# Moving VectorE's low-part subtraction to an earlier place within an attention step

## The chip, the cores and the metric

The kernel runs on 1 core of a Trainium2 chip. The metric is the device time of one launch in microseconds (us). The shown time is a median of 3 runs. The profile is of one further execution, with its own time.

## What is computed

The reference is two blocks of two layers each on one sequence of 512 positions, width 1024, in float32. Three of its attentions matter here, since the same class of the kernel computes all three:

- the sparse attention of the first block's second layer: 16 heads of 64, causal, with a mask made by a top-128 choice and a relative bias; its output is multiplied by silu(z);
- the sliding-window attention of the second block's first layer: 16 heads, window 128, with sinks;
- the second block's second layer, where two attentions of 16 heads (selected blocks, which here are all of them, and a window of 512) are added with gates to a compressed one.

```python
def attention(q, k, v, bias, mask):
    s = einsum(q, k) + bias
    s = where(mask, s, NEG_INF)
    p = softmax(s)
    return einsum(p, v)
...
x = x + (out * gate) @ w_out
```

Each output is then the input of a projection, `@ w_out`. The kernel keeps float32 precision in that projection by splitting a tile x into a rounded high part (`hi`, type fp32r) and a low part `lo = x - hi`, and by adding three products: hi times the weights' low part, lo times their high part, hi times their high part.

## The kernel before

The program is written engine by engine. Each stage is a class with one method per engine (`on_pe`, `on_dve`, `on_act`, `on_pool`, `on_sp`), and the five instruction streams meet only at semaphores. An engine takes its own stream strictly in the order in which it is written, so a wait holds back all that stands behind it on that engine.

The class `Attention` is used three times. In this text its uses are called the causal block (it writes `odd_hi`, `odd_lo`; 641 to 721 us of the trace), the windowed block (`win_hi`, `win_lo`; 822 to 881 us) and the two-branch block (`long_hi`, `long_lo`; 1393 to 1531 us). The 16 heads are taken in 8 pairs (m = 0 to 7), the 512 queries in 4 tiles of 128 in the order t = 3, 1, 2, 0. One pair and one query tile (and one branch) is a step s: 32 steps in the causal and the windowed block (4 a pair), 64 in the two-branch block (8 a pair). How many keys a step reads goes by its tile: 512, 256, 384 and 128 for t = 3, 1, 2, 0 in the causal and two-branch blocks, at most 256 in the windowed one.

The engines run a software pipeline over the steps. A step's work is, in order:

- PE `score(s)` (line 2000; mask added by line 1997): two heads' scores into one of two pairs of banks. It waits for the logits of step s-2.
- DVE `logit(s)` (line 2068; with sinks a small copy first, line 2065): scores plus bias from the bank into a probability buffer, with the row minimum.
- ACT `exp(s)` (line 2161), then DVE `share(s)` (line 2074, a reciprocal), then POOL `divide(s)` (line 2133).
- PE `turn(s)` (line 2014), three steps later: transposes of the probabilities. It waits for POOL.
- `keep(s)`: the transposed probabilities from the bank to SBUF, on ACT (line 2170) for even steps, on DVE (line 2096) for odd ones; in the two blocks with more than 256 keys DVE takes the rest of the even ones (line 2098).
- PE `mix(s)` (line 2031), five steps later: probabilities times values into bank 7. It waits for `finish(s-1)`, since all steps use the same bank for their sum.
- DVE `finish(s)` (lines 2084, 2086, 2088), six steps later: the sum is read from bank 7 and put into the output tile `out(m)`.
- ACT `split_high(m)` (line 2174), after the last `finish` of the pair: `hi(m) = round(out(m))`.
- DVE `split_low(m)` (line 2102), one step later on DVE: `lo(m) = out(m) - hi(m)`. It waits for `split_high(m)`.

With the constants FINISH = 6, HIGH = 6 and LOW = 7, `split_low(m)` stands in DVE's step s = 10 + 4m of the causal and windowed blocks and s = 14 + 8m of the two-branch block. In that step DVE's stream also has `finish(s-6)`, `logit(s)` of a tile t = 2, `share(s-1)` and `keep(s-3)`, and the next step begins with `finish(s-5)`, for which PE's `mix(s-4)` waits. Steps from 32 (64) on have no logit; only the splits of m = 6 and m = 7 lie there in the first two blocks, and only that of m = 7 in the third. ACT's step 9 + 4m is `exp`, `keep`, `split_high(m)`.

The waits that carry this text:

```python
# PE, mix(s)
pe.wait_ge(self.outs.sem, self.outs.at(s if s < self.NS - 3 else s - 1))
# DVE, split_low(m)
dve.wait_ge(self.high.sem, self.high.at(m + 1))
# ACT, split_high(m)
act.wait_ge(self.outs.sem, self.outs.at(self.per_pair * (m + 1)))
```

The `lo` tiles are read only by the output projection behind the block (`part_ready`), whose first products start at the end of the block.

Of the kernel before, what the change touches and what calls it, by code (L numbers as in the profile page):

```python
# [76 lines left out]
class Stage:  # L77
# [11 lines left out]
    def on_dve(self, dve):  # L89
        pass  # L90
# [1815 lines left out]
class Attention(Stage):  # L1906
# [144 lines left out]
    def on_dve(self, dve):  # L2051
        nc, steps, keys, st, pad = self.k.nc, self.steps, self.keys, self.st, self.pad

        def logit(s):
            m, t, e = steps[s]
            nk = keys(t)[1]
            pr, b = self.probs_of[s % 4], self.bias_of(s)
            if self.bias is not None and s % self.per_pair == 0:
                dve.wait_ge(self.landed[m % 2].sem, self.landed[m % 2].at((m // 2 + 1) * 16))
            if t in self.pooled:  # L2060
                dve.wait_ge(self.added.sem, self.added.at(2 * m + t))
            dve.wait_ge(self.turned.sem, self.turned.at(s - 3))
            dve.wait_ge(self.scores.sem, self.scores.at(s + 1))
            if self.sink is not None:
                nc.vector.tensor_copy(pr[:, :, 0], self.sink[:, 2 * m:2 * m + 2])
            for x in range(2):
                first = -CUT if self.sink is None else self.sink[:, 2 * m + x:2 * m + x + 1]
                nc.vector.tensor_tensor_reduce(out=pr[:, x, pad:pad + nk], in0=self.S(s, x)[:, 0:nk], in1=b[:, x, :],  # L2068
                                               scale=1.0, scalar=first, op0=ALU.add, op1=ALU.min,
                                               accum_out=st[:, s % 4, 0, x:x + 1]).then_inc(self.logits.sem, 1)  # L2070

        def share(s):
            dve.wait_ge(self.probs.sem, self.probs.at((s + 1) * 2))
            nc.vector.reciprocal(st[:, s % 4, 2, :], st[:, s % 4, 1, :]).then_inc(self.dens.sem, 1)  # L2074

        def finish(s):
            m, t, e = steps[s]
            r = slice(t * P, (t + 1) * P)
            o = self.out(m)[:, r]
            dve.wait_ge(self.mixed.sem, self.mixed.at(s + 1))  # L2080
            if self.finishing is not None and s % self.per_pair == 0:
                self.finishing(dve, m)
            if self.add:
                nc.vector.tensor_tensor(o, self.O(s), o, ALU.add).then_inc(self.outs.sem, 1)
            elif self.times is not None:
                nc.vector.tensor_tensor(o, self.O(s), self.times(m)[:, r], ALU.mult).then_inc(self.outs.sem, 1)
            else:
                nc.vector.tensor_copy(o, self.O(s)).then_inc(self.outs.sem, 1)

        def keep(s):  # L2090
            blocks = keys(steps[s][1])[2]
            r, w = blocks[0][1], 2 * P * len(blocks)
            dve.wait_ge(self.mixed.sem, self.mixed.at(s - 1))
            dve.wait_ge(self.turned.sem, self.turned.at(s + 1))
            if s % 2 == 1:
                nc.vector.tensor_copy(self.turned_of[1][0:r, 0:w], self.T[1][0:r, 0:w]).then_inc(self.kept[1].sem, 1)
            else:
                nc.vector.tensor_copy(self.turned_of[0][0:r, 512:w], self.T[0][0:r, 512:w]).then_inc(self.rest.sem, 1)

        def split_low(m):  # L2100
            dve.wait_ge(self.high.sem, self.high.at(m + 1))
            nc.vector.tensor_tensor(self.lo(m), self.out(m), self.hi(m).bitcast(F32), ALU.subtract).then_inc(self.low.sem, 1)

        for s in range(self.NS + self.LOW):
            if 0 <= s - self.FINISH < self.NS:
                finish(s - self.FINISH)
            if s < self.NS:
                logit(s)
            if 0 <= s - 1 < self.NS and not (self.trail and s == 2):
                share(s - 1)  # L2110
            if self.first_dve is not None and s < 2:
                self.first_dve(dve, s)
            if self.trail and s == 1:
                share(1)
            if self.trail and s == 2:
                self.before.evict(dve, "dve", self.before.tiles - 1)
            if 0 <= s - self.TURN < self.NS and (self.halves or (s - self.TURN) % 2 == 1):
                keep(s - self.TURN)
            done = s - self.LOW + 1
            if done > 0 and done % self.per_pair == 0:  # L2120
                split_low(done // self.per_pair - 1)

    def on_pool(self, pool):
        nc, steps, keys, pad = self.k.nc, self.steps, self.keys, self.pad
# [1019 lines left out]
```

## Time and profile before

| what | value |
|---|---|
| median of 3 runs | 1942.56 us (1942.49 to 1942.62) |
| the profiled execution's own time | 1942.33 us |
| its span, first to last instruction | 1940.5 us |
| granted TensorE clock, mean | 0.999 |
| PE busy | 1910.1 us, 98% |
| DVE busy | 1071.6 us, 55% |
| ACT busy | 770.6 us, 40% |
| POOL busy | 333.0 us, 17% |
| DVE line 2102, causal block | 8 times, median 872 ns |
| DVE line 2102, windowed block | 8 times, median 692 ns |
| DVE line 2102, two-branch block | 8 times, median 682 ns |

PE, PEld, DVE, ACT and POOL are TensorE's matmuls, its weight loads, VectorE, ScalarE and GpSimd. Busy shares are means over the whole span; in a timeline, a row's start plus its duration can lie up to some 0.1 us behind the start of the next row on the same engine, because the next instruction enters before the last has left. Times in brackets behind a row are the engine's idle time before it and who ended it. The profiled execution lies 1.8 us above its span and 0.2 us below the median of the runs.

### The profile page before, as it was taken

To read this page: it belongs to the slowest core of one execution; us is meant where nothing else is said; L and a number is where in the kernel's file an instruction comes from. 1 tells how busy PE (TensorE), PEld (TensorE's weight loads), DVE (VectorE), ACT (ScalarE), POOL (GpSimd) and SP (SyncE) were. 2 spreads that over 40 slices of the span, in tenths; PEclk is the share of its full clock that TensorE was granted. 3 is DMA by queue.
4 is the path that set the end of the run, shared out by engine and by line. 5 is a ranking of instruction groups with operands and counts; after the bars stand their busy time and mean duration, and the time that the engine had idled before them with its cause. 6 is when DMAs were issued, how large, how long until landed. Compare 5 with 4: busy or idle time off the path is not lost.

```text
span 1940.5 us, 25271 instructions
## 1 busy us (share of the span) xinstructions
PE 1910.1 (98%) x9688; PEld 1505.5 (78%) x9688; DVE 1071.6 (55%) x2029; ACT 770.6 (40%) x1407; POOL 333.0 (17%) x419
## 2 busy tenths in 40 slices
PE   9999999999999999999999999999999999999998
PEld 7887778888777668758888888888766788888886
DVE  5576644444699765485544443353788654544323
ACT  4343333432454654474322222232567442222213
POOL 0640000001130751051000000030256310000002
PEclk9999999999999999999999999999999999999999
DMA  9452324443323123312333333365100133333332
GB/s 206 135 171 75 101 85 152 141 152 86 101 68 104 47 56 87 93 50 87 98 96 95 95 96 94 101 172 171 44 2 1 45 98 96 100 98 98 98 98 77
DMA packets 297246, 187.67 MB, mean 97 GB/s; under 512 B 32543, under 2 KB 274719, under 8 KB 296870
## 3 DMA queue, kind: packets, MB, share of 16 engines
q1 hardware_dynamic: 288958, 168.02, 30.6%
q10 hardware_dynamic: 8168, 18.03, 2.4%
q8 instruction: 78, 1.28, 0.3%
q14 instruction: 42, 0.34, 0.1%
HBM read 183.79 MB, written 17.96 MB: 104 GB/s over the span
## 4 chain that ended last, share of the span: by engine, by line
PE 87%; DVE 8%; ACT 2%; issue 2%; DMA 1%; POOL 0%; ACTq 0%; DVEq 0%; SPq 0%
PE banks L298 21%; PE banks L300 20%; PE banks L299 20%; PE banks L2031 3%; PE banks L2000 3%; PE banks L2014 2%; PE banks L599 2%; PE banks L600 2%; PE banks L598 2%; PE banks L412 2%; PE banks L414 2%; PE banks L413 2%; PE banks L950 1%; DVE idx_score L1216 1%; PE banks L958 1%
## 5 line engine op out<-in xcount | busy, mean ns | idle before, releaser
L2396 DVE TENSOR_TENSOR wlo<-raw,whi 128x1024 fp32r<-128x1024 f32 (+1 forms) x281 | 360.8, 1285 | 320.0 <-ACT whi L2387 319.5
L298 PE MATMUL banks<-xs,wlo 128*128 128x512 f32 x1336 | 531.9, 398 | 0.1
L300 PE MATMUL banks<-xs,whi 128*128 128x512 f32 x1336 | 520.6, 390 | 0.0
L299 PE MATMUL banks<-xs,whi 128*128 128x512 f32 x1336 | 520.3, 389 | 0.0
L2387 ACT ACTIVATE whi<-raw 128x1024 fp32r<-128x1024 f32 (+1 forms) x281 | 293.1, 1045 | 249.1 <-PE banks L300 94.6
L298 PEld LDWEIGHTS banks<-xs,wlo 128*128 128x128 f32 x1336 | 250.9, 188 | 60.6 <-issue 7.5
L299 PEld LDWEIGHTS banks<-xs,whi 128*128 128x128 f32 x1336 | 251.0, 188 | 54.1 <-issue 3.4
L300 PEld LDWEIGHTS banks<-xs,whi 128*128 128x128 f32 x1336 | 250.8, 188 | 52.7
L524 POOL TENSOR_TENSOR squares<-squares,x_tmp 128x512 f32<-128x512 f32 x35 | 46.9, 1339 | 715.5 <-ACT x_tmp L516 715.5
L2133 POOL TENSOR_SCALAR prob<-prob,long_stat,gt_s 128x512 f32<-128x512 f32 (+3 forms) x128 | 80.2, 636 | 129.8 <-DVE long_stat L2074 129.7
L2960 ACT ACTIVATE a_hi<-ff_tmp 128x512 fp32r<-128x512 f32 x44 | 27.8, 632 | 166.2 <-DVE ff_tmp L2959 166.2
L2957 ACT ACTIVATE ff_tmp<-ff_tmp 128x512 f32<-128x512 f32 x44 | 27.8, 632 | 165.7 <-DVE ff_tmp L2956 165.7
L2161 ACT ACTIVATE prob<-prob,long_stat 128x512 f32<-128x512 f32 (+3 forms) x128 | 70.7, 553 | 41.0 <-DVE long_stat L2068 40.6
L2421 ACT ACTIVATE xs<-hT,gains 128x512 fp32r<-128x512 f32 x40 | 28.9, 723 | 134.2 <-DVE hT L2416 111.1
L2014 PEld LDWEIGHTS banks<-ident,prob 128*128 128x128 f32 x432 | 45.8, 141 | 40.6 <-issue 36.2
L412 PE MATMUL banks<-wlo,xs 128*128 128x512 f32 x192 | 75.0, 391 | 0.3 <-DVE wlo L2396 0.3
L414 PE MATMUL banks<-whi,xs 128*128 128x512 f32 x192 | 74.7, 389 | 0.0
L413 PE MATMUL banks<-whi,xs 128*128 128x512 f32 x192 | 74.7, 389 | 0.0
L2959 DVE TENSOR_TENSOR ff_tmp<-banks,ff_tmp 128x512 f32<-128x512 f32 x44 | 30.4, 692 | 78.1 <-PE banks L300 78.1
L2956 DVE TENSOR_TENSOR ff_tmp<-banks,row_scale 128x512 f32<-128x512 f32 x44 | 30.4, 691 | 75.9 <-PE banks L300 75.8
L678 POOL TENSOR_TENSOR tok_scaled<-tok,last_gain 128x512 f32<-128x512 f32 x8 | 10.3, 1284 | 353.6 <-DVE tok L656 353.6
L2014 PE MATMUL banks<-ident,prob 128*128 128x128 f32 x432 | 68.0, 285 | 2.1 <-ACT pT L2170 1.0
(402 smaller groups left out, 3207.7 us busy)
## 6 DMA issues: line engine op xcount, KB each, us to landing
raw<-in_ffn_w_gu SPq DMA_DIRECT2D x88, 512.0 KB, 3.8
raw<-in_e_w_in SPq DMA_DIRECT2D x56, 512.0 KB, 3.9
raw<-in_ffn_w_down SPq DMA_DIRECT2D x38, 512.0 KB, 3.6
s_skew<-s_bias ACTq DMA_DIRECT2D x6, 2560.0 KB
raw<-in_o_w_in SPq DMA_DIRECT2D x21, 512.0 KB, 4.0
raw<-in_e_w_out SPq DMA_DIRECT2D x16, 512.0 KB, 3.9
raw<-in_b_w_in SPq DMA_DIRECT2D x15, 512.0 KB, 3.9
raw<-in_a_w_qkv SPq DMA_DIRECT2D x10, 512.0 KB, 4.0
```

Source lines behind the costliest of these rows:

```text
L298: nc.tensor.matmul(out, k.wlo[:, chunk.slot, at, :], self.x_hi(kt), start=first, stop=False)
L299: nc.tensor.matmul(out, k.whi[:, chunk.slot, at, :], self.x_lo(kt), start=False, stop=False)
L300: ins = nc.tensor.matmul(out, k.whi[:, chunk.slot, at, :], self.x_hi(kt), start=False, stop=last)
L412: nc.tensor.matmul(out, self.x_hi(kt)[:, r], rest[:, b, :], start=kt == 0, stop=False)
L413: nc.tensor.matmul(out, self.x_hi(kt)[:, r], high[:, b, :], start=False, stop=False)
L414: ins = nc.tensor.matmul(out, self.x_lo(kt)[:, r], high[:, b, :], start=False, stop=kt == MT - 1)
L2000: ins = nc.tensor.matmul(S(s, x)[:, 0:nk], self.q[r, m, t * P:(t + 1) * P], self.key(e, m, x)[r, k0:k0 + nk], start=not masked, stop=True)
L2014: ins = nc.tensor.transpose(T[s % 2][0:r, (2 * b + x) * P:(2 * b + x + 1) * P], self.probs_of[s % 4][:, x, self.pad + b * P:self.pad + b * ...
L2133: nc.gpsimd.tensor_scalar(pr, pr, self.st[:, s % 4, 2, x:x + 1], g, ALU.mult, ALU.mult).then_inc(self.ready.sem, 1)
L2161: nc.scalar.activation(pr, pr, ACT.Exp, bias=st[:, s % 4, 0, x:x + 1], scale=-1.0, accum_out=st[:, s % 4, 1, x:x + 1]).then_inc(self.probs ...
L2387: self.nc.scalar.activation(self.whi[:, chunk.slot, 0:chunk.blocks, :], self.raw[:, chunk.slot, 0:chunk.blocks, :], ACT.Copy).then_inc(sel ...
L2396: self.nc.vector.tensor_tensor(self.wlo[:, chunk.slot, 0:chunk.blocks, :], self.raw[:, chunk.slot, 0:chunk.blocks, :], hi.bitcast(F32), AL ...
```

## The change

`split_low` moves within DVE's step: it stood last, and now stands between `finish` and `logit`. Nothing is added, removed or resized, and no wait is changed.

```diff
         for s in range(self.NS + self.LOW):
             if 0 <= s - self.FINISH < self.NS:
                 finish(s - self.FINISH)
+            done = s - self.LOW + 1
+            if done > 0 and done % self.per_pair == 0:
+                split_low(done // self.per_pair - 1)
             if s < self.NS:
                 logit(s)
             if 0 <= s - 1 < self.NS and not (self.trail and s == 2):
...
             if 0 <= s - self.TURN < self.NS and (self.halves or (s - self.TURN) % 2 == 1):
                 keep(s - self.TURN)
-            done = s - self.LOW + 1
-            if done > 0 and done % self.per_pair == 0:
-                split_low(done // self.per_pair - 1)
```

DVE's stream in the causal block, step 10, as it was. L2086 is `finish`, L2068 `logit` (each with its read of the row minimum; the number behind a name is that of its buffer), L2074 `share`, L2096 `keep`, L2102 `split_low`:

```order
L2086 TENSOR_TENSOR zT_191<-banks,zT_191 128x128
L2068 ISA prob_216,odd_stat_204<-banks,bias_masked_197 128x384
L2068 ISA odd_stat_204 128x1
L2068 ISA prob_216,odd_stat_204<-banks,bias_masked_197 128x384
L2068 ISA odd_stat_204 128x1
L2074 RECIPROCAL odd_stat_204<-odd_stat_204 128x2
L2096 COPY pT_217<-banks 128x256
L2102 TENSOR_TENSOR odd_lo_215<-zT_191,odd_hi_214 128x512
L2086 TENSOR_TENSOR zT_191<-banks,zT_191 128x128
```

And now:

```order
L2086 TENSOR_TENSOR zT_191<-banks,zT_191 128x128
L2102 TENSOR_TENSOR odd_lo_215<-zT_191,odd_hi_214 128x512
L2068 ISA prob_216,odd_stat_204<-banks,bias_masked_197 128x384
L2068 ISA odd_stat_204 128x1
L2068 ISA prob_216,odd_stat_204<-banks,bias_masked_197 128x384
L2068 ISA odd_stat_204 128x1
L2074 RECIPROCAL odd_stat_204<-odd_stat_204 128x2
L2096 COPY pT_217<-banks 128x256
L2086 TENSOR_TENSOR zT_191<-banks,zT_191 128x128
```

The subtraction has gone ahead of two logits, a reciprocal and a copy; it is still ahead of the next `finish`. The same holds for m = 0 to 5 here.

DVE's stream in the windowed block, step 10, now (L2065 is the copy of the sinks, L2088 is `finish`):

```order
L2088 COPY oT_185<-banks 128x128
L2102 TENSOR_TENSOR win_lo_227<-oT_185,win_hi_226 128x512
L2065 COPY prob_228<-win_small_186 128x2
L2068 ISA prob_228,win_stat_224<-banks,win_bias_223,win_small_186 128x256
L2068 ISA win_stat_224 128x1
L2068 ISA prob_228,win_stat_224<-banks,win_bias_223,win_small_186 128x256
L2068 ISA win_stat_224 128x1
L2074 RECIPROCAL win_stat_224<-win_stat_224 128x2
L2096 COPY pT_229<-banks 128x256
L2088 COPY oT_185<-banks 128x128
```

Before, the L2102 row stood between the last two rows; again for m = 0 to 5. In the two-branch block it is so for m = 0 to 6.

At the end of the causal block, step 34 (m = 6), where no logit is left:

```order
L2098 COPY pT_217<-banks 128x256
L2086 TENSOR_TENSOR zT_191<-banks,zT_191 128x128
L2102 TENSOR_TENSOR odd_lo_215<-zT_191,odd_hi_214 128x512
L2096 COPY pT_217<-banks 128x256
L2086 TENSOR_TENSOR zT_191<-banks,zT_191 128x128 x3
```

There the subtraction has gone ahead of one copy, L2096, only; the windowed block ends likewise. The last split of each block (m = 7) has the same place as before. PE, ACT, POOL and SP have the same streams as before.

## Rows read from the trace of the kernel before

**Rows 1.** The page's chain of work that ended last, shares of the span by engine.
```profile
PE 87%; DVE 8%; ACT 2%; issue 2%; DMA 1%; POOL 0%; ACTq 0%; DVEq 0%; SPq 0%
```
**Rows 2.** Waits of PE: line, releaser, us in total, times, longest us.
```profile
PE banks L2031 <- DVE oT L2088: 4.9, 7, 0.8
PE banks L2031 <- DVE zT L2086: 3.1, 9, 0.7
...
PE banks L2031 <- DVE oT L2084: 0.4, 1, 0.4
```
**Rows 3.** Timeline of DVE, causal block, steps 10 and 11: start, duration, operation, idle before.
```profile
656.58 0.28 DVE L2086 TENSOR_TENSOR zT<-banks,zT 128x128 f32<-128x128 f32 x1
657.22 0.56 DVE L2068 CUSTOM_DVE_ANT_0 prob<-banks,bias_masked 128x384 f32<-128x384 f32 x1 [0.36 <-PE banks L2000]
...
658.26 0.40 DVE L2096 COPY pT<-banks 128x256 f32<-128x256 f32 x1
658.58 0.87 DVE L2102 TENSOR_TENSOR odd_lo<-zT,odd_hi 128x512 fp32r<-128x512 f32 x1
659.38 0.28 DVE L2086 TENSOR_TENSOR zT<-banks,zT 128x128 f32<-128x128 f32 x1
```
**Rows 4.** Timeline of ACT at the same place.
```profile
657.24 0.62 ACT L2174 ACTIVATE odd_hi<-zT 128x512 fp32r<-128x512 f32 x1
```
**Rows 5.** Timeline of PE at the same place.
```profile
658.35 1.09 PE L2014 MATMUL banks<-ident,x_tmp 128*128 128x128 f32 x8
659.71 0.88 PE L2031 MATMUL banks<-pT,vt 128*64 128x128 f32 x12 [0.27 <-DVE zT L2086]
```
**Rows 6.** Timeline of DVE, windowed block, steps 14 and 15 (m = 1).
```profile
836.98 0.26 DVE L2088 COPY oT<-banks 128x128 f32<-128x128 f32 x1
837.56 0.17 DVE L2065 COPY prob<-win_small 128x2 f32<-128x2 f32 x1 [0.32 <-PE banks L2000]
...
839.14 0.69 DVE L2102 TENSOR_TENSOR win_lo<-oT,win_hi 128x512 fp32r<-128x512 f32 x1 [0.21 <-ACT win_hi L2174]
839.75 0.28 DVE L2088 COPY oT<-banks 128x128 f32<-128x128 f32 x1
```
**Rows 7.** Timeline of ACT, windowed block.
```profile
838.49 0.62 ACT L2174 ACTIVATE win_hi<-oT 128x512 fp32r<-128x512 f32 x1
```
**Rows 8.** Timeline of PE, windowed block.
```profile
840.09 0.66 PE L2031 MATMUL banks<-pT,vt_w 128*64 128x128 f32 x8 [0.68 <-DVE oT L2088]
...
841.31 0.66 PE L2014 MATMUL banks<-ident,win_prob 128*128 128x128 f32 x4
```
**Rows 9.** Timeline of POOL, windowed block.
```profile
838.71 1.47 POOL L2133 TENSOR_SCALAR win_prob<-win_prob,win_stat 128x256 f32<-128x256 f32 x2 [0.62 <-DVE win_stat L2074]
```
**Rows 10.** Timeline of DVE, two-branch block, steps 22 and 23 (m = 1).
```profile
1430.43 0.56 DVE L2068 CUSTOM_DVE_ANT_0 prob<-banks,bias_all 128x384 f32<-128x384 f32 x1 [0.33 <-PE banks L2000]
...
1431.79 0.68 DVE L2102 TENSOR_TENSOR long_lo<-oT,long_hi 128x512 fp32r<-128x512 f32 x1
1432.39 0.28 DVE L2084 TENSOR_TENSOR oT<-banks,oT 128x128 f32<-128x128 f32 x1
```
**Rows 11.** Timeline of ACT, two-branch block.
```profile
1430.47 0.62 ACT L2174 ACTIVATE long_hi<-oT 128x512 fp32r<-128x512 f32 x1
```
**Rows 12.** Timeline of DVE, end of the causal block, step 34.
```profile
717.47 0.42 DVE L2096 COPY pT<-banks 128x256 f32<-128x256 f32 x1 [0.34 <-PE banks L2031]
717.81 0.68 DVE L2102 TENSOR_TENSOR odd_lo<-zT,odd_hi 128x512 fp32r<-128x512 f32 x1
```
**Rows 13.** Timeline of ACT, end of the causal block.
```profile
717.01 0.62 ACT L2174 ACTIVATE odd_hi<-zT 128x512 fp32r<-128x512 f32 x1
```
**Rows 14.** Timeline of POOL, causal block.
```profile
658.44 1.36 POOL L2133 TENSOR_SCALAR squares<-squares,odd_stat 128x256 f32<-128x256 f32 x2 [1.05 <-DVE odd_stat L2074]
```
**Rows 15.** Busy time by stretch: us, PE, PEld, DVE, ACT, POOL busy, clock, DMA share, GB/s.
```profile
840.00:860.00 20.00, 18.55 (x160) 11.24 (x161) 17.31 (x87) 14.40 (x51) 10.58 (x23) 1.00 0.29 76
1920.00:1940.00 20.00, 13.16 (x59) 10.55 (x57) 8.95 (x24) 9.50 (x24) 10.27 (x8) 0.91 0.28 106
```

## The prediction

> **What bounds the kernel now.** I began with the page's chain of work that ended last: 87% of the span is PE, 8% is DVE [rows 1]. So a delay of another engine costs time only where PE waits for it. Next, PE's waits: PE line 2031 (`mix`) waits for DVE's `finish` 4.9 us in all in the windowed block (line 2088), 3.1 us in the causal block (line 2086), 0.4 us in the two-branch block (line 2084) [rows 2]. These are the places at which the moved subtraction can act, since `finish` is the DVE instruction behind it. Then I read the timelines of all engines around one split in each block.
>
> Causal block. DVE ends `finish(4)` at 656.86, is idle 0.36 us for PE's scores, and does `logit(10)` from 657.22, the copy from 658.26, the split from 658.58 (0.87 us) and `finish(5)` from 659.38 [rows 3]. PE's transposes have been entering since 658.35; `mix(6)` starts at 659.71 after 0.27 us of idle time, released by that `finish` [rows 5]. So PE waits here already, and whatever moves `finish(5)` later from here moves PE one for one. The windowed block has the same picture with 0.68 us of idle time, `mix` starting at 840.09 behind a `finish` that starts at 839.75 [rows 6, 8]. The pattern repeats at every split, every 9.62 us and every 7.40 us. In the two-branch block `finish(17)` starts at 1432.39 behind the split [rows 10], and PE's waits there come to a single listed one of 0.4 us [rows 2], so at the splits it waits less than the listing shows; 0.1 us a split is my estimate.
>
> **What the split waits for.** It needs the high part from ACT. In the causal block ACT makes that from 657.24 for 0.62 us, to 657.86 [rows 4]. At its old place, 658.58, the split never waited. At the new place DVE is free at 656.86 and must stand idle 1.0 us for it. In the windowed block the high part is ready at 838.49 + 0.62 = 839.11 [rows 7] while `finish` ends at 837.24 [rows 6]: 1.9 us. There the old split already waited 0.21 us [rows 6]. In the two-branch block the high part is ready at 1431.09 [rows 11] and `logit` started at 1430.43 [rows 10]. Behind the waiting split now stand the two logits, the reciprocal for POOL, the copy of an odd step's transposes and `finish`. ACT's time does not come forward: its instructions before the high part hang on earlier logits and on PE's transposes, neither of which the change moves against PE.
>
> **The sum.** For each split I let DVE start it 0.03 us after ACT's end (839.11 to 839.14) [rows 6, 7], and keep the rest of DVE's order with its old durations.
>
> *Causal.* Split at 657.86 + 0.03 = 657.89. For its length there are two rows: 0.87 us at the old place, where a POOL instruction was running from 658.44 [rows 3, 14], and 0.68 us at the block's end, where POOL has no work [rows 12]. At 657.89 POOL is idle too: its row says it had been idle 1.05 us before 658.44 [rows 14], and with the change its next work starts only after the `share` behind the split. I take 0.68, after which the next instruction entered 0.60 later. `logit(10)` then starts at 658.49 instead of 657.22, +1.27. All up to the copy's end shifts by that, so `finish(5)` starts at 658.58 + 1.27 = 659.85 instead of 659.38: +0.47 us. With 0.87 it would be +0.67.
>
> The Trainium skill (SBUF — State Buffer, the section with the single rule on the shared port pair) says that a VectorE instruction with two SBUF inputs and a GpSimd instruction that reads SBUF exclude each other, and that the one that comes second waits. By that rule the split would have 0.68 us here and the sum is the one below; if 0.87 were its own length, the sum would be 1.2 us more. The rows agree with it in sign, though 0.19 us is less than a full wait for the 1.36 us that POOL spends.
>
> *Windowed.* Split at 839.14, next instruction 0.61 later (839.14 to 839.75) [rows 6]: sink copy and `logit` at 839.75 instead of 837.56, +2.19. DVE was busy from 837.56 to 838.93 (839.14 less 0.21 idle) [rows 6], 1.37 us, less the 0.08 us by which a next instruction overlaps a copy's end. `finish` starts at 839.75 + 1.29 = 841.04 instead of 839.75: +1.29 us.
>
> *Two-branch.* Split at 1431.09 + 0.03 = 1431.12, next at +0.60: 1431.72 instead of 1430.43, +1.29. `finish` was due at 1431.79 without the split, so it starts at 1433.08 instead of 1432.39: +0.69 us.
>
> *Ends.* The split of m = 6 in the first two blocks passes only a copy. Causal: high part at 717.01 + 0.62 = 717.63 [rows 13], split at 717.66, copy at 718.26 with 0.34 us (717.47 to 717.81), `finish` at 718.60; before, 717.81 + 0.60 = 718.41 [rows 12]. +0.19 us. I take the same for the windowed block. The split of m = 7 doesn't move: 0.
>
> Counts: causal 6 x 0.47 + 0.19 = 3.0; windowed 6 x 1.29 + 0.19 = 7.9; two-branch 7 x 0.69 = 4.8. Sum **+15.7 us**. Nothing gives it back: PE is busy otherwise, so each `mix` that starts late ends the block late, and the projection's products stand behind it in PE's queue. The `lo` tile is ready earlier, which nobody waited for. The profiled execution took 1942.33 us, so it would take 1958.0; the median lies 0.23 us higher, which gives **1958.3 us**.
>
> **Whether the late logits cost more than the late finish.** They hold back exp, `share`, POOL's `divide` and PE's `turn` two PE steps later. Windowed block, the tightest: `share` shifts by 2.19 us, POOL's work of 838.71 + 1.47 = 840.18 [rows 9] to 842.37. PE's `turn` behind it started at 841.31 [rows 8] and is itself shifted by 1.29 to 842.60. It still has 0.2 us to spare, and more if POOL's 1.47 us shrinks now that the split isn't beside it. I cost this at nothing.
>
> **The rivals.**
>
> *A. A filled gap (faster).* DVE is idle 0.36 us before `logit` in the causal block and 0.32 in the windowed one [rows 3, 6]; a split there would use that time and free `finish`, and PE's waits at the splits, 6 x 0.27 + 6 x 0.68 + 7 x 0.1 = 6.4 us, would go: 1942.6 - 6.4 = 1936.2 us. It decides from the point where the high part is ready when `finish` ends, or about 0.5 us later in the causal block. The rows put it 1.0 and 1.9 us later [rows 3, 4, 6, 7]. Chance 0.02.
>
> *B. The delay is taken up (within 0.2%).* If PE reached `mix` late for reasons of its own, or ACT got ahead of DVE once PE is slower, only a fraction would be left, 0 to 3.9 us: 1944 us or so. PE's idle time in front of `mix` before the change speaks against it [rows 5, 8]. Chance 0.03.
>
> *C. POOL's chain decides (slower still).* If POOL's instructions get longer or exp starts later than I think, `turn` waits as well in the windowed block. With 0.5 us more than my 842.37, less the 0.2 to spare, that is 6 x 0.3 = 1.8 us: 1960.1 us. Chance 0.10.
>
> *D. TensorE's clock.* PE's idle time per 7.40 us pair of the windowed block grows from 0.68 to 1.97 us. The granted clock was 1.00 with 18.55 of 20 us busy in the middle of that block, and 0.91 in the one stretch with 13.16 us busy, the kernel's last [rows 15]; the new block lies between them, 77% busy. At 0.91, PE's 6.7 us of work a pair would take 0.66 us more, 6 times: 4.0 us, 1962.3 us; chance 0.04. The Trainium skill (TensorE: Matmul & The Clock Gate, "A second HAM failure mode: psum-queue depth-cycling") tells of a kernel whose short idle times between groups of matmuls made the clock swing between its levels; no row here shows that for gaps of this size.
>
> **How the numbers follow.** My forecast, +15.7 us, has chance 0.81, and its own bounds: with 0.87 us for the causal splits 1959.5; with 0.1 us less per split, 19 of them, for semaphore times and overlaps that I read only to some hundredths, 1956.4. The range takes in C and half of the way to D above, and below a case in which one block in three costs a good half of what I say (the two-branch block, -2.5 us): 1955.0 to 1961.5. A difference under 0.2%, 3.9 us, is about what a measurement of this kernel can't tell from no change. Faster by more than that: 0.02 (A). Within it: 0.03 (B). Slower: 0.95.
>
> **What would show it.** In the profile of the changed kernel, DVE's wait of lines 2102 for ACT line 2174 should be the new one: about 1.0 us at each of the 6 causal and 7 two-branch splits and 1.9 at each of the 6 windowed ones. PE's waits of line 2031 for `finish` should rise to some 0.74, 1.97 and 0.8 us a split. The pairs should take 10.1 and 8.7 us instead of 9.62 and 7.40. The causal split should last 0.68 us. Line 2014's wait for POOL should stay small. PE's waits unchanged would make the forecast wrong, or a wait of line 2102 that is near zero, or a clock below 1.00 in the windowed block.

## The result and the profile after

| | median, us | ratio to before, 95% interval |
|---|---|---|
| before | 1942.59 (1942.49 to 1942.84, 4 runs) | |
| the change | 1963.08 (1961.94 to 1964.22, 4 runs) | 1.0105 (1.0092 to 1.0117) |

The change costs 20.5 us. The forecast was +15.7 us and its range ended at 1961.5: the direction was right, the size was not, and the time lies 1.6 us outside. The profiled execution took 1963.01 us with a span of 1961.2 us and a mean granted clock of 0.993, against 0.999 before.

DVE's timeline of the causal block, step 10 and the start of step 11 (start, duration, idle time before; compare [rows 3]):

```profile
656.66 0.28 DVE L2086 TENSOR_TENSOR zT<-banks,zT 128x128 f32<-128x128 f32 x1
657.97 0.69 DVE L2102 TENSOR_TENSOR odd_lo<-zT,odd_hi 128x512 fp32r<-128x512 f32 x1 [1.02 <-ACT odd_hi L2174]
658.58 0.55 DVE L2068 CUSTOM_DVE_ANT_0 prob<-banks,bias_masked 128x384 f32<-128x384 f32 x1
...
659.61 0.40 DVE L2096 COPY pT<-banks 128x256 f32<-128x256 f32 x1
659.93 0.28 DVE L2086 TENSOR_TENSOR zT<-banks,zT 128x128 f32<-128x128 f32 x1
```

The split stands idle for 1.02 us. PE's timeline shows what comes of it in the causal and the two-branch block (compare [rows 5]):

```profile
658.43 1.09 PE L2014 MATMUL banks<-ident,x_tmp 128*128 128x128 f32 x8
660.27 0.88 PE L2031 MATMUL banks<-pT,vt 128*64 128x128 f32 x12 [0.74 <-DVE zT L2086]
...
1449.85 0.88 PE L2031 MATMUL banks<-pT,vt_s 128*64 128x128 f32 x12 [0.75 <-DVE oT L2084]
```

PE waits 0.74 us where it waited 0.27. Now PE's timeline in the windowed block (compare [rows 8]):

```profile
843.15 0.66 PE L2014 MATMUL banks<-ident,win_prob 128*128 128x128 f32 x4
845.75 0.66 PE L2031 MATMUL banks<-pT,vt_w 128*64 128x128 f32 x8 [1.95 <-DVE oT L2088]
846.34 0.86 PE L2000 MATMUL banks<-kT_w,qT_w 64*128 64x256 f32 x4
847.12 1.12 PE L2014 MATMUL banks<-ident,win_prob 128*128 128x128 f32 x4
...
851.00 1.12 PE L2031 MATMUL banks<-pT,vt_w 128*64 128x128 f32 x8
...
854.75 0.66 PE L2014 MATMUL banks<-ident,win_prob 128*128 128x128 f32 x4
```

It waits 1.95 us instead of 0.68, and then the same groups of four transposes take 1.12 us instead of 0.66 for some 7 us. The busy time by stretch says why; behind the length, PE's busy time and count come the granted clock, the DMA share and GB/s:

```profile
844.00:846.00 2.00, 0.25 (x4) 1.00 0.00 0
846.00:848.00 2.00, 2.00 (x16) 0.69 0.27 46
848.00:850.00 2.00, 2.00 (x11) 0.50 0.25 85
850.00:852.00 2.00, 2.00 (x14) 0.50 0.02 4
852.00:854.00 2.00, 2.00 (x12) 0.60 0.00 0
854.00:856.00 2.00, 1.87 (x24) 1.00 0.00 0
...
862.00:864.00 2.00, 0.23 (x3) 0.95 0.00 0
864.00:866.00 2.00, 1.82 (x12) 0.50 0.16 14
...
872.00:874.00 2.00, 2.00 (x14) 0.50 0.00 0
874.00:876.00 2.00, 2.00 (x20) 0.98 0.00 0
...
884.00:886.00 2.00, 2.00 (x15) 0.57 0.00 0
886.00:888.00 2.00, 2.00 (x5) 0.57 0.00 0
888.00:890.00 2.00, 2.00 (x10) 1.00 0.00 0
```

0.50 is TensorE's lower level, 1.2 of 2.4 GHz. It was granted in three stretches, called dips below, each right behind one of PE's idle times of about 1.9 us: 846 to 853, 864 to 874 and 884 to 887 us. Before the change the granted clock was 1.00 in every stretch from 820 to 890 us; one of them stands in [rows 15].

Where the 20.5 us went can be read from the splits' own starts. The last causal split starts at 723.39 instead of 720.23, +3.2 us. From it to the last windowed one (896.09, before 880.40) there are 12.5 us more, and from there to the last one of the two-branch block (1551.3, before 1530.7) 4.9 us more. Against my terms of 3.0, 7.9 and 4.8 us, 4.6 of the 4.9 us that I missed lie in the windowed block.

### The profile page after: what moved, and what is told of

Same layout as the page of the kernel before. It is cut to its first block, busy times and chain, and to the rows that moved or that the text cites. A ratio compares the mean times of both kernels' runs of the same rounds, so it can differ in the third digit from the quotient of the medians.

```text
span 1961.2 us, 25271 instructions
## 1 busy us (share of the span) xinstructions
PE 1919.9 (98%) x9688; PEld 1511.3 (77%) x9688; DVE 1071.3 (55%) x2029; ACT 769.9 (39%) x1407; POOL 324.3 (17%) x419
## 4 chain that ended last, share of the span: by engine, by line
PE 88%; DVE 7%; ACT 2%; issue 1%; DMA 1%; POOL 0%; ACTq 0%; DVEq 0%; SPq 0%
PE banks L298 20%; PE banks L300 20%; PE banks L299 20%; PE banks L2031 4%; PE banks L2000 4%; PE banks L2014 3%; PE banks L598 2%; PE banks L600 2%; PE banks L599 2%; PE banks L412 2%; PE banks L414 2%; PE banks L413 2%; DVE prob L2068 1%; PE banks L950 1%; DVE idx_score L1216 1%
## 5 line engine op out<-in xcount | busy, mean ns | idle before, releaser
L678 POOL TENSOR_TENSOR tok_scaled<-tok,last_gain 128x512 f32<-128x512 f32 x8 | 10.3, 1287 | 353.6 <-DVE tok L656 353.6
```

## The experiments

The theory after the result: the late `finish` costs what the sum says in each block, and TensorE's clock, which falls because of the 1.95 us idle time, costs the rest, in the windowed block alone. The rival: the missing time comes from something common to all three blocks (a longer instruction, a slower semaphore), and the clock's dips are hidden.

**One block at a time.** The early place is used under a condition, the old one otherwise:

```diff
+            early = self.times is not None
             done = s - self.LOW + 1
-            if done > 0 and done % self.per_pair == 0:
+            if early and done > 0 and done % self.per_pair == 0:
                 split_low(done // self.per_pair - 1)
...
+            if not early and done > 0 and done % self.per_pair == 0:
+                split_low(done // self.per_pair - 1)
```

`self.times` picks the causal block, `self.add` the two-branch block, `self.sink` the windowed one.

> The early place is used in the causal block alone. Theory (each block pays its own late finish, and the rest of the 20.5 us is TensorE's clock in the windowed block): +3.1 us, 1945.7, granted clock 1.00 throughout the attention, PE idle 0.74 us at each of the six splits. Rival (the 4.8 us that my sum missed lie in all three blocks in proportion): 20.5 x 3.0/15.7 = +3.9 us, 1946.5.

Measured: 1945.46 us, beside 1942.48 for before, ratio 1.0015 (1.0006 to 1.0024): +3.0 us. PE is idle 0.74 us at the splits, and the clock is 1.00 throughout the attention. The profiled execution took 1947.21 us, the longest of its runs, and has a dip of the clock of its own, long before the attention; the last section comes back to it.

> The early place is used in the two-branch block alone. Theory: +4.9 us, 1947.5, clock 1.00 in that block, PE idle about 0.8 us at each of the seven splits. Rival (the missing time lies in all blocks in proportion): 20.5 x 4.8/15.7 = +6.3 us, 1948.9.

Measured: 1947.42 us, 1.0026 (1.0017 to 1.0036): +4.9 us, with PE idle 0.74 us at the splits and the clock at 1.00.

> The early place is used in the windowed block alone. Theory: +7.9 us of late finish and some 4.6 us of clock, +12.5 us, 1955.1, with stretches at 0.5 of the clock between the splits of that block. Rival (missing time in proportion, no clock effect): 20.5 x 7.9/15.7 = +10.3 us, 1952.9.

Measured: 1955.95 us (1953.35 to 1957.29), 1.0067 (1.0054 to 1.0079): +13.5 us. The three add up to 21.4 us, against 20.5 for all together. The rival's 10.3 us for the windowed block lie outside that interval; its 3.9 and 6.3 us for the other two lie inside theirs, but the medians and the starts of the splits in the changed kernel's trace (+3.2 and +4.9 us) are at the theory's numbers. The windowed stretches of this kernel, PE's busy time and clock as above:

```profile
842.00:846.00 4.00, 3.12 (x20) 0.68 0.27 66
846.00:850.00 4.00, 4.00 (x22) 0.50 0.01 2
...
870.00:874.00 4.00, 3.69 (x22) 0.60 0.02 4
874.00:878.00 4.00, 4.00 (x21) 0.55 0.00 0
```

Its profiled execution has two dips where that of the change has three, and a span of 1951.6 us, below the median of the runs, which spread by 3.9 us. How many dips an execution gets is not fixed.

**The gap filled.** In the changed kernel PE gets work that nobody reads, inside the idle time:

```diff
+            if self.sink is not None and s >= 6 and s % 4 == 2 and s < self.NS - 3:
+                for _ in range(8):
+                    nc.tensor.transpose(self.k.banks[:, 5, 0:P], self.k.ident[:, :], self.k.ident[:, :])
             pe.wait_ge(self.outs.sem, self.outs.at(s if s < self.NS - 3 else s - 1))
```

> The changed kernel, and in the windowed block PE does eight transposes of the identity into an unused bank ahead of the mix that waits, at six places: about 1.0 us of work inside the idle 1.95 us, which delays nothing. They add work whose result nobody reads. Theory (the clock costs about 4.6 us because of that idle time): no stretch of the windowed block below 1.00, and 1963.1 - 4.6 = 1958.5 us. Rival (the clock's dips are hidden in DVE's waits and cost nothing, or come from something else than the idle time): 1963 us, dips stay or go.

Measured: 1958.08 us (1957.89 to 1958.25), 1.0079 (1.0065 to 1.0093). This is 5.0 us less than the changed kernel, though DVE, ACT and POOL do the same and PE does more; the longest run here, 1958.25, lies 3.7 us below the shortest of the changed kernel, 1961.94. PE's timeline and the stretches of the windowed block (the added lines shift the numbers by 3: line 2026 is the added transposes, 2034 `mix`, 2091 `finish`):

```profile
835.21 1.04 PE L2026 MATMUL banks<-ident 128*128 128x128 f32 x8
837.31 0.66 PE L2034 MATMUL banks<-pT,vt_w 128*64 128x128 f32 x8 [1.07 <-DVE oT L2091]
```

```profile
844.00:854.00 10.00, 8.43 (x75) 1.00 0.11 29
854.00:864.00 10.00, 8.35 (x76) 1.00 0.09 26
864.00:874.00 10.00, 8.93 (x78) 1.00 0.48 134
```

No stretch is below 1.00. The splits in this block start every 8.63 us, all six alike, and the last windowed split comes 56.3 us after the first, in the changed kernel 61.2. So the dips do cost, and they are gone when PE has work in the gap. What is left, 15.6 us over before, agrees with the 15.7 that I had worked out.

**Half filled.** The same with `range(4)`.

> As the filled gap, with four transposes instead of eight: about 0.5 us of work in the idle 1.95 us, leaving PE idle some 1.4 us (before the change 0.68, in the changed kernel 1.95, with eight some 0.9). If the clock falls in proportion to the idle time, half of the 4.6 us comes back: 1960.5 us. If it falls only beyond some amount of idle time between 0.9 and 1.95 us, then either none (1963) or all (1958.1) comes back. A result nobody reads is added.

Measured: 1958.14 us (1958.02 to 1959.85), 1.0079 (1.0066 to 1.0092). All of it comes back, with PE idle 1.51 us:

```profile
837.23 0.66 PE L2034 MATMUL banks<-pT,vt_w 128*64 128x128 f32 x8 [1.51 <-DVE oT L2091]
```

```profile
844.00:854.00 10.00, 7.49 (x66) 1.00 0.10 27
854.00:864.00 10.00, 7.98 (x72) 1.00 0.11 28
```

The cost doesn't grow in proportion to the idle time: at 1.51 us a pair there is none, at 1.95 us there is all of it. What it is about the gap that counts stays open: four transposes make the single idle time shorter and PE's busy time in the pair longer at once, and no run changes one of the two alone.

**The wait without the logits behind it.** In all three blocks the split stands behind `logit` instead of ahead of it:

```diff
-            done = s - self.LOW + 1
-            if done > 0 and done % self.per_pair == 0:
-                split_low(done // self.per_pair - 1)
             if s < self.NS:
                 logit(s)
+            done = s - self.LOW + 1
+            if done > 0 and done % self.per_pair == 0:
+                split_low(done // self.per_pair - 1)
```

> The split stands between logit and share of the same step, in all three blocks: same work, but the wait for ACT holds back no logits. Theory (what costs is the standing wait for the high part, not the order as such): causal, the high part is ready before the logits end, nothing is waited for, and the split is no longer beside POOL's work, 0.69 instead of 0.87 us: finish 0.19 us earlier, 6 times, -1.1; windowed, the logits end at 838.5, the high part comes at 839.1, so share and copy stand behind the wait and finish comes 0.40 us later than before, 6 times, +2.4; two-branch 0; ends +0.4. Sum +1.7, 1944.2 us, clock 1.00 with PE idle 1.1 us at the windowed splits. Rival (any split before share and keep costs what the changed kernel costs): 1955 us or more.

Measured: 1943.79 us (1943.56 to 1945.37), 1.0006 (0.9997 to 1.0015), the clock at 1.00 in all stretches. DVE and PE in the windowed block:

```profile
838.58 0.69 DVE L2102 TENSOR_TENSOR win_lo<-oT,win_hi 128x512 fp32r<-128x512 f32 x1 [0.59 <-ACT win_hi L2174]
```

```profile
839.92 0.66 PE L2031 MATMUL banks<-pT,vt_w 128*64 128x128 f32 x8 [1.05 <-DVE oT L2088]
```

The two logits now use the time in which ACT makes the high part, so DVE's wait is down to 0.59 us and PE's to 1.05. A place ahead of `share` and `keep` is cheap by itself; what costs is a wait that holds back the logits too.

**A step later.** The changed kernel with one constant changed:

```diff
-    TURN, MIX, FINISH, HIGH, LOW = 3, 5, 6, 6, 7
+    TURN, MIX, FINISH, HIGH, LOW = 3, 5, 6, 6, 8
```

> The split keeps the changed kernel's place between finish and logit, but one step later (LOW = 8), where the high part is ready about 1 us before and finish of the next step has gone ahead of it. Theory: DVE's wait for ACT is gone, PE's waits at the splits (6 x 0.27 + 6 x 0.68 + 7 x 0.1 = 6.4 us) go as well, and about 0.5 us at each end of the first two blocks: 1942.5 - 7.4 = 1935.1 us, clock 1.00. Rival (a split between finish and logit costs because of the late logits, wherever its high part stands): slower than before, 6 x 0.6 us or more in the windowed block, 1946 us.

Measured: 1934.37 us (1934.13 to 1935.7), beside 1942.60 for before: 0.9958 (0.9944 to 0.9972). It is 8.2 us faster than before and 28.7 us faster than the change. DVE and PE in the windowed block:

```profile
835.63 0.28 DVE L2088 COPY oT<-banks 128x128 f32<-128x128 f32 x1
835.91 0.69 DVE L2102 TENSOR_TENSOR win_lo<-oT,win_hi 128x512 fp32r<-128x512 f32 x1
836.52 0.16 DVE L2065 COPY prob<-win_small 128x2 f32<-128x2 f32 x1
```

```profile
835.53 0.66 PE L2014 MATMUL banks<-ident,win_prob 128*128 128x128 f32 x4
836.12 0.66 PE L2031 MATMUL banks<-pT,vt_w 128*64 128x128 f32 x8
```

The split waits for nobody, `finish` has gone ahead of it, and PE goes from its transposes to `mix` without a gap. It stands between `finish` and `logit` exactly as in the change, but its high part is there. Two things differ from the change, the operand that is ready and the `finish` that has gone ahead, and this run doesn't tell what each of them gives.

## Why the prediction was partly wrong

- **The split would wait for ACT, 1.0 and 1.9 us.** Right: 1.02, 1.89 and 1.03 us in the three blocks, but for the two windowed splits whose pair ran with the clock down (0.86 and 0.85 us).
- **The causal term, 6 x 0.47 + 0.19.** Right: PE's wait rose by 0.47 us, the splits are 10.10 us apart instead of 9.62, and the block alone costs 3.0 us.
- **The causal split at 0.68 us instead of 0.87.** Right: 0.69 at all eight, and POOL's pair beside the old place takes 0.94 us instead of the 1.36 of [rows 14].

```profile
659.79 0.94 POOL L2133 TENSOR_SCALAR squares<-squares,odd_stat 128x256 f32<-128x256 f32 x2 [2.31 <-DVE odd_stat L2074]
```

- **The two-branch term, 7 x 0.69.** Right: 4.9 us alone.
- **The windowed term, 6 x 1.29 + 0.19 = 7.9.** Its mechanism and size held only for the late `finish`: with the gap filled, the splits are 8.63 us apart, 1.23 more than before, and the whole change costs 15.6 us, against the 15.7 of the sum.
- **Rival D, the clock, chance 0.04, 4.0 us.** This is the step that failed. It was named with its place, but I took it for unlikely and put it at nothing in the sum, and the range ended at 1961.5, short of its 1962.3. A clock below 1.00 in the windowed block was among the signs named against the forecast, and it came. The measured cost is 5.0 us (1963.08 less 1958.08). I judged it by PE's busy share, 77%, between a stretch at 1.00 and one at 0.91 [rows 15]. The stretch at 0.91 can't carry that. Taken apart (length, PE busy and count, clock, DMA share, GB/s), its clock is 1.00 as long as PE works, and lower only behind the program's last matmul:

```profile
1925.00:1930.00 5.00, 5.00 (x23) 1.00 0.36 132
1930.00:1935.00 5.00, 3.16 (x14) 1.00 0.43 163
1935.00:1940.00 5.00, 0.00 (x0) 0.66 0.34 129
```

So no row of before had matmuls at a lower clock. Nor had one an idle time like the new one. A split's wait grew from 0.68 to 1.95 us, and the longest single idle time of PE before the change, up to its last matmul, was 1.49 us, once, at a clock of 1.00:

```profile
1386.54 1.16 PE L1716 MATMUL banks<-few_pT,value_blocks 64*128 64x128 f32 x16 [1.49 <-DVE oT L1899]
```

An unknown that no row covers deserved more than 0.04. The price was low as well: I spread a mean of 0.91 over the block, while in fact three stretches of 3 to 10 us ran at half the clock. Part of that was hidden, since DVE's wait for ACT shrinks in a pair with the clock down:

```profile
853.32 0.69 DVE L2102 TENSOR_TENSOR win_lo<-oT,win_hi 128x512 fp32r<-128x512 f32 x1 [0.86 <-ACT win_hi L2174]
...
861.96 0.69 DVE L2102 TENSOR_TENSOR win_lo<-oT,win_hi 128x512 fp32r<-128x512 f32 x1 [1.89 <-ACT win_hi L2174]
```

- **The range.** The parts named for it don't give its ends. Half of D's 4.0 us above 1958.3 is 1960.3; 1961.5 comes out only if that half is put on the 1959.5 of long causal splits. The case of the two-branch block, -2.5 us, is 1955.8 and not 1955.0.
- **Rival A, a filled gap.** Its point of decision, a high part that is ready when `finish` ends, fits the kernel with the split a step later: 8.2 us faster, where A's waits came to 6.4 and my expectation with the blocks' ends to 7.4. The change doesn't reach that point.
- **Rival C, POOL's chain.** PE's waits for POOL before `turn` stayed what they were, two of 0.4 us in the whole program.

## What to carry to other kernels

An instruction that is moved ahead in an in-order engine is worth its place only if its operand is there at the new time: compare the end of its producer with the time at which the engine gets there, and add what is queued behind the wait. A step later can be the better place, because it lets the instruction that others wait for go first. And when a change makes TensorE's single idle times longer than any in the trace (here 1.49 us), the clock is an open term of the sum, of several us here, and not a remote case.

## What the runs showed of the hardware that was not expected

- The clock fell to 1.2 GHz with PE idle once for 1.95 us in 8.63 us, and stayed at 2.4 GHz with the idle time cut to 1.51 us and the same pair length. Not each such idle time is followed by a dip: in the profiled execution of the change four splits have one of about 1.9 us (the other two come in slow pairs, where PE arrives late), and three dips follow. The times follow suit: four runs of the changed kernel lie 2.3 us apart, four with the gap filled 0.4.
- A long idle time isn't the only thing behind which the clock falls. In the profiled execution of the causal block alone, it fell to 0.50 near the kernel's start, where no idle time of PE in the 20 us before was above 0.68 us. In the profile of before the same place is at 1.00. What set this dip off no run shows:

```profile
26.00:28.00 2.00, 1.89 (x8) 0.77 0.58 27
28.00:30.00 2.00, 2.00 (x6) 0.50 0.69 5
30.00:32.00 2.00, 2.00 (x9) 0.87 0.86 6
```

- The work put into the gap was transposes only, and with four of them (0.60 us of PE's time) the clock stayed at 1.00. The Trainium skill (TensorE: Matmul & The Clock Gate, "Part 4: PE-mode transpose") says that a transpose doesn't count as busy for the clock in the same way as a matmul. No run here tells how they count, since none put plain matmuls in their place.
- In the causal block, VectorE's subtraction of two SBUF tensors and GpSimd's two scalings of another one both took longer where they overlapped: 0.87 against 0.69 us and 1.36 against 0.94 us. In the windowed block only GpSimd's did: beside the old place they took 1.47 us [rows 9], now 0.94, while the subtraction took 0.69 us in both [rows 6]. There it had started 0.43 us behind the first scaling (838.71 to 839.14), in the causal block 0.14 us (658.44 to 658.58).
